# Weight-block sums of the seven-product chunks made by accumulating transfers instead of VectorE; parameter rows on GpSimd's queue; chunk 6 transposed two products later

## The reference, cut to what matters

```
def swiglu(h, w_gate, w_up, w_down):
    return (jax.nn.silu(h @ w_gate) * (h @ w_up)) @ w_down
for layer in range(DEPTH):
    x = x + 0.5 * swiglu(rmsnorm(x, norm_g[layer, 0]), ffn_w_gate[layer, 0], ffn_w_up[layer, 0], ffn_w_down[layer, 0])
    x = x + hybrid_mixer(rmsnorm(x, norm_g[layer, 1]), ...)
    x = x + 0.5 * swiglu(rmsnorm(x, norm_g[layer, 2]), ffn_w_gate[layer, 1], ffn_w_up[layer, 1], ffn_w_down[layer, 1])
```

## Time and profile before

| | |
|---|---|
| median of three runs | 2633.23 us |
| profiled execution, its own time | 2632.9 us |
| its span in the trace | 2631.2 us |
| TensorE busy | 2583.8 us, 98% |
| VectorE busy | 1801.3 us, 68% |
| ScalarE busy | 1555.4 us, 59% |
| GpSimd busy | 833.4 us, 32% |
| SyncE's DMA queue | 443.25 MB, 56.2% of 16 engines' span |
| mean granted TensorE clock | 0.997 |

### The profile page before, as it was taken

The page is one execution under the profiler, slowest core; times in us unless marked ns, Lnnn a source line. Parts: engine busy times, 40 slices in busy tenths (PEclk is TensorE's granted clock), DMA queues, the critical chain, the costliest instruction groups (busy, mean ns, idle before and its releaser), DMA issues.

```text
span 2631.2 us, 42862 instructions
## 1 busy us (share of the span) xinstructions
PE 2583.8 (98%) x16554; PEld 2242.2 (85%) x16554; DVE 1801.3 (68%) x2641; ACT 1555.4 (59%) x2202; POOL 833.4 (32%) x415
## 2 busy tenths in 40 slices
PE   9999999999999998999999999999999999999999
PEld 8888998888888996888789999978878899999787
DVE  6873745877863735876876787458768767873686
ACT  5665655656565654655565645656565657456655
POOL 0007671000018671000007754720000087548100
PEclk9999999999999999999999999999999999999999
DMA  9545547547535446548547742585475487325752
GB/s 290 176 129 181 146 156 252 177 143 247 179 124 182 147 161 215 168 151 250 178 126 174 172 91 80 167 255 179 137 249 179 109 191 171 82 82 179 246 184 97
DMA packets 349166, 447.19 MB, mean 170 GB/s; under 512 B 29612, under 2 KB 238512, under 8 KB 348964
## 3 DMA queue, kind: packets, MB, share of 16 engines
q1 hardware_dynamic: 348148, 443.25, 56.2%
q10 hardware_dynamic: 816, 1.21, 0.2%
HBM read 443.31 MB, written 1.05 MB: 169 GB/s over the span
## 4 chain that ended last, share of the span: by engine, by line
PE 84%; ACT 5%; DVE 4%; SPq 2%; issue 2%; DMA 2%; POOL 0%; DVEq 0%; ACTq 0%; POOLq 0%
PE PS L614 25%; PE PS L616 25%; PE PS L615 25%; PE PS L867 1%; SPq L403 1%; ACT wp L638 1%; DMA ring<-in_ffn_w_in_dram 1%; ACT xh L1498 1%; PE PS L1288 1%; DMA ring<-in_ffn_w_up_dram 1%; PE PS L1361 1%; DVE sq L2313 1%; PE PS L1351 1%; ACT wp L674 1%; PE PS L819 1%
## 5 line engine op out<-in xcount | busy, mean ns | idle before, releaser
L646 POOL TENSOR_TENSOR wp<-ring,wp 128x1024 fp32r<-128x1024 f32 (+2 forms) x332 | 786.1, 2384 | 1482.1 <-ACT wp L638 1481.6
L638 ACT ACTIVATE wp<-ring 128x1024 fp32r<-128x1024 f32 x712 | 746.6, 1054 | 570.7 <-PE PS L614 363.5
L646 DVE TENSOR_TENSOR wp<-ring,wp 128x1024 fp32r<-128x1024 f32 x380 | 459.1, 1220 | 209.4 <-ACT wp L638 208.8
L614 PE MATMUL PS<-wp,xh 128*128 128x512 f32 (+2 forms) x1440 | 568.2, 395 | 14.5 <-DVE wp L646 13.3
L616 PE MATMUL PS<-wp,xl 128*128 128x512 f32 (+2 forms) x1440 | 558.3, 388 | 0.0
L615 PE MATMUL PS<-wp,xh 128*128 128x512 f32 (+2 forms) x1312 | 507.6, 387 | 0.0
L614 PE MATMUL PS<-xh,wp 128*128 128x256 f32 x1536 | 445.0, 290 | 0.8 <-POOL wp L646 0.7
L616 PE MATMUL PS<-xh,wp 128*128 128x256 f32 x1536 | 434.4, 283 | 0.0
L615 PE MATMUL PS<-xl,wp 128*128 128x256 f32 x1536 | 434.3, 283 | 0.0
L614 PEld LDWEIGHTS PS<-wp,xh 128*128 128x128 f32 x1440 | 270.9, 188 | 78.4 <-DVE wp L646 17.9
L614 PE MATMUL PS<-wp,hh 128*128 128x512 f32 x832 | 328.4, 395 | 0.0
(11 more groups left out here) (342 smaller groups left out, 3508.0 us busy)
## 6 DMA issues: line engine op xcount, KB each, us to landing
ring<-in_mix_w_in_dram SPq DMA_DIRECT2D x256, 256.0 KB, 3.8
ring<-in_ffn_w_in_dram SPq DMA_DIRECT2D x224, 256.0 KB, 3.5
ring<-in_ffn_w_down_dram SPq DMA_DIRECT2D x176, 256.0 KB, 3.6
ring<-in_w_in_dram SPq DMA_DIRECT2D x176, 256.0 KB, 3.0
ring<-in_ffn_w_out_dram SPq DMA_DIRECT2D x176, 256.0 KB, 3.8
W<-in_ffn_w_in_dram SPq DMA_DIRECT2D x64, 512.0 KB, 6.9
ring<-in_ffn_w_gate_dram SPq DMA_DIRECT2D x112, 256.0 KB, 3.2
ring<-in_ffn_w_up_dram SPq DMA_DIRECT2D x112, 256.0 KB, 3.8
```

The costliest lines, as they stand in the source:

```text
L614: first_ = mm(o, w[0], x[0], start=start, stop=False, skip_group_check=True)
L638: act_(dst, src, ACT.Copy).then_inc(hi_ready, 1)
L646: (engine or v_).tensor_tensor(dst, src, part_views(t, wh)[0], ALU.subtract).then_inc(lo[t.slot()], 1)
```

## The change

The four subtractions L2313 go from VectorE. In their place ScalarE makes a negated copy of b11 in t1's buffer and of b22 in t2's (`negated`, two operations of 128x2048 in each pair), and GpSimd's queue issues four accumulating transfers of 1 MB within on-chip memory in each pair (`pool_sums`), each of which waits for the one before: t1 = -b11 + b12; then b12's buffer becomes t3 = b12 - b22; then t2 = -b22 + t1; then, once both halves of the low part of M6 are made, the same buffer becomes t4 = t2 + b21. The signs of t2 and t3 are turned, and those of the activations' sums with them. t4's own buffer goes. The four sums now have semaphores of their own, on which the high parts wait.

The negated copies of the first pair stand on ScalarE in the rounds of chunks 3 and 4, those of the second pair after down tiles 6 and 8. SyncE's wait before block b21 is now for M4. `load_params2` goes to GpSimd's queue, after the low parts of the last mixer of the first block and before the sums of that feed-forward's first pair; the sums of its second pair stand behind GpSimd's constants, so behind the wait for L1442's transposes. `turn(PLAIN - 1)` stands between M3 and M7 and ScalarE's and VectorE's `turned(c - 1)` behind the high and low parts of M2.

```
 def two_chunks(p):                                   # TensorE
                 product("M5", sum_part(1, 1), True)
-                if p == 0:
-                    turn(PLAIN - 1)
...
                 product("M3", sum_part(1, 0))
+                if p == 0:
+                    turn(PLAIN - 1)
...
+            def negated(p, dst, src):                 # ScalarE
+                e.wait_ge(blocks_in[src], blocks_landed(s, p))
+                act_(raw[dst], raw[src], ACT.Copy, scale=-1.0).then_inc(ff[1].sem, ff[1].did(f"{tag}.{dst}n.{p}"))
...
                 chunk(c)
+                if c == 3:
+                    negated(0, "t1", "b11")
                 if c == 4:
                     sums_high()
                 high(e, t, 2)
+                if c == 4:
+                    negated(0, "t2", "b22")
...
-            high(e, t, 4)
+            high(e, t, 2)
+            negated(1, "t1", "b11")
+            high(e, t, 2)
+            negated(1, "t2", "b22")
...
             low_whole(0, "M1")                        # VectorE
             turned(PLAIN - 2)
-            low_whole(0, "M5", "T2")
-            block3(0)
-            block4(0)
+            low_whole(0, "M5")
             two_chunks(0, *PAIRS[0])
...
+        def pool_sums(e, t, ff, s, tag, p):           # GpSimd
+            at = blocks_landed(s, p)
+            add = lambda n, dst, src: e.dma_start(raw[dst], raw[src], accum_op=ALU.add).then_inc(summed_in[n], 16)
+            t.k = PAIR_AT[p]
+            e.wait_ge(ff[1].sem, ff[1].at(f"{tag}.t1n.{p}"))
+            e.wait_ge(blocks_in["b12"], at)
+            add("t1", "t1", "b12")
+            e.wait_ge(ff[1].sem, ff[1].at(f"{tag}.t2n.{p}"))
+            e.wait_ge(summed_in["t1"], at // 2)
+            add("t3", "b12", "t2")
+            e.wait_ge(summed_in["t3"], at // 2)
+            add("t2", "t2", "t1")
+            e.wait_ge(summed_in["t2"], at // 2)
+            e.wait_ge(blocks_in["b21"], at)
+            for i in range(2):
+                low_ready(e, t, SUM_OF["M6"] + i)
+            add("t4", "t2", "b21")
...
             e.wait_ge(first["mix"][2].sem, first["mix"][2].at("mc3"))
+            load_params2(e)
+            pool_sums(e, f1, ff, stage1(lay, 2), "f1", 0)
             ok(p_.memset(tmask[:], 0.0))
...
                 ok(p_.memset(DU["U", c][half[1], :, half[0]], 0.0), "masks" if c == 1 else None)
+            pool_sums(e, f1, ff, stage1(lay, 2), "f1", 1)
```

More of the change, by code:

```diff
@@ L445, in pair_block @@
                     sp.wait_ge(track_[0].sem, track_[0].at(f"{tag_}.{product}.{p_}", lay_))
-                    if name == "b21":
-                        sp.wait_ge(track_[2].sem, track_[2].at(f"{tag_}.T4.{p_}", lay_))
                 load_block(sp, p, name, gate, up)
-            blocks = (("b11", "M1"), ("b12", "M7"), ("b22", "M3"), ("b21", "M2"))
+            blocks = (("b11", "M1"), ("b12", "M7"), ("b22", "M3"), ("b21", "M4"))
             for c in range(PLAIN):
@@ L506, in _ @@
                                 load_tile(sp, t, a[key][lay][c * P:(c + 1) * P, :])
-                    def between(last=lay == LAYERS - 1 and half == 1):
-                        if last:
-                            load_params2(sp)
                     load_ffn(sp, t, first["ffn"], f"f{half}", lay, kmajor(a["ffn_w_gate"][lay, half]),
                              kmajor(a["ffn_w_up"][lay, half]), a["ffn_w_down"][lay, half],
-                             (first["mix"], lay) if half == 1 else None, before, between)
+                             (first["mix"], lay) if half == 1 else None, before, lambda: None)
                     before = (first["ffn"], f"f{half}", lay, 1)
@@ L657, in sum_ready @@
             else:
-                e.wait_ge(ff[2].sem, ff[2].at(f"{tag}.{RAW_OF[n].upper()}.{p}"))
+                e.wait_ge(summed_in[RAW_OF[n]], blocks_landed(s, p) // 2)
         def by_planes(ap):
@@ L2293, in sums3 @@
                 own("S1")
-                v_.tensor_tensor(sq[:, front, q1], sq[:, front, q0], sq[:, front, q1], ALU.subtract).then_inc(
+                v_.tensor_tensor(sq[:, front, q1], sq[:, front, q1], sq[:, front, q0], ALU.subtract).then_inc(
                     ff[2].sem, ff[2].did(f"{tag}.S3"))
@@ L2298, in sums2 @@
                 own("S3")
-                v_.tensor_tensor(sq[:, front, q0], sq[:, back, q1], sq[:, front, q0], ALU.subtract).then_inc(
+                v_.tensor_tensor(sq[:, front, q0], sq[:, front, q0], sq[:, back, q1], ALU.subtract).then_inc(
                     ff[2].sem, ff[2].did(f"{tag}.S2"))
@@ L2303, in sums4 @@
                 own("S2")
-                v_.tensor_tensor(sq[:, back, q0], sq[:, back, q0], sq[:, front, q0], ALU.subtract).then_inc(
+                v_.tensor_tensor(sq[:, back, q0], sq[:, back, q0], sq[:, front, q0], ALU.add).then_inc(
                     ff[2].sem, ff[2].did(f"{tag}.S4"))
@@ L2310, in sums_low, with low_whole @@
                     ff[2].sem, ff[2].did(f"{tag}.sl{i}"))
[L2312 to L2339, removed]
+            def low_whole(p, n):
+                if n == "M5":
+                    e.wait_ge(summed_in["t2"], blocks_landed(s, p) // 2)
                 low_sum(e, t, n).then_inc(lo[t.slot(SUM_OF[n])], 1)
@@ L2401, in dve_ffn @@
                 chunk(c)
[L2402 to L2412, removed]
+            low(e, t, FRONT - 5)
+            low_whole(1, "M1")
+            low_whole(1, "M5")
             two_chunks(1, *PAIRS[1])
@@ L2960, in _ @@
             env.lay = 0
+        def pool_sums(e, t, ff, s, tag, p):
[15 more added lines that the diff above has]
+            add("t4", "t2", "b21")
         def pool_mix2(e, t):
+            ff = second["ffn"]
             low(e, t, 4 if env.lay else 2, nc.gpsimd)
+            for p in range(len(PAIRS)):
+                pool_sums(e, t, ff, stage2(env.lay, 0), "f0", p)
             t.k = FFN_TILES
@@ L2990, in pool_mix2 @@
             low(e, t, 3 * KB - AHEAD + 4, nc.gpsimd)
+            t.k = T2 - FFN_TILES
+            f1 = Tiles(t.number())
+            for p in range(len(PAIRS)):
+                pool_sums(e, f1, ff, stage2(env.lay, 2), "f1", p)
         @block.gpsimd
@@ L3016, in _ @@
                     low(e, t, 2, nc.gpsimd)
+                ff, f1 = first["ffn"], Tiles((lay + 1) * T1 - FFN_TILES)
+                for p in range(len(PAIRS)):
+                    pool_sums(e, t, ff, stage1(lay, 0), "f0", p)
                 t.k = FFN_TILES
                 low(e, t, T1 - 2 * FFN_TILES + 2, nc.gpsimd)
+                if lay < LAYERS - 1:
+                    for p in range(len(PAIRS)):
+                        pool_sums(e, f1, ff, stage1(lay, 2), "f1", p)
             e.wait_ge(first["mix"][2].sem, first["mix"][2].at("mc3"))
+            load_params2(e)
+            pool_sums(e, f1, ff, stage1(lay, 2), "f1", 0)
             ok(p_.memset(tmask[:], 0.0))
```

29 lines of the change are left out of this document (15 added, 14 removed).

## The result

The changed kernel takes 2677.4 us (median of 4 runs, 2675.9 to 2690.7) against 2633.4; the ratio is 1.0171 with a 95% interval of 1.0139 to 1.0203. It is slower by 44 us where I forecast 15 us faster.

The account below looks back on a forecast made before the run. The prediction took TensorE to bound the kernel, busy 2583.8 of 2631.2 us. Its sum was 2632.9 - 11.8 - 14.3 + 5 + 4 + 2 = 2617.8, said as 2618 us, range 2606 to 2665, likeliest case 2613 to 2628.

Parts of the forecast that it names:

- What can be won: TensorE's waits at chunk 6's transposes (11.8 us) and the gap from SyncE's parameter rows (14.3 us): 26.1 us together.
- The 1.48 us go even if the transposes stayed: Chunk 6, eight feed-forwards: without two VectorE subtractions, `gated` ends early enough to end each wait, 11.8 us in all.
- 5 + 4: Second pairs: 5 us lost over eight feed-forwards to slow transfers, 4 us more in the first block's last one.
- First pair ... Loss 0: First pairs, before M4: t4 has 10.3 us, from 93.7 to 104.0, and may take 10, so nothing is lost.
- The clock: TensorE's granted clock falls behind long gaps; expected with transfers at 11 us, no term in the sum.
- rival A: Accumulating transfers too slow, TensorE waits before M6 and M4 of the second pairs: slower, 2655 at 9.6 us each; chance 0.28.
- The price L of a transfer: Time of one 1 MB accumulating transfer: 7.9 us alone, 8.6 beside the weights, with 5 and 11 kept as bounds.
- 4L - 33.1: Loss in each second pair: four transfers against 33.1 us of room before M4; forecast 0.6 us each, 5 in all.
- The late chain behind GpSimd's constants: First block's last feed-forward: the second pair's sums start behind GpSimd's two constants, costing 4 us more.
- break-even of 8.3: Mean transfer time in us over a second pair's four, from which rival A decides.
- C: Parameter rows do as much harm from GpSimd's queue, so only 11.8 us are gained: 2630, no change; chance 0.09.
- D: VectorE keeps GpSimd from preparing transfers, starts up to 2.3 us late, 10.2 us each at worst: 2675; chance 0.04.

Follow-up runs that it names:

- params_only: The kernel before with one edit, the 28 parameter rows moved from SyncE's queue to GpSimd's: 2620.8 us, 0.9952.
- plain_copies: The changed kernel with its 64 accumulating transfers made plain copies, additions left out, so a price and no result: 2606.4 us, 0.9894.
- sums_earlier_turn_first: As sums_earlier, but chunk 6's transposes stay between M5 and M6 as in the kernel before: 2608.4 us, 0.9903.
- params_turn: The kernel before with parameter rows on GpSimd's queue and chunk 6's transposes between M3 and M7, all sums still on VectorE: 2618.0 us, 0.9938.
- sums_earlier: params_turn with the first pair's four sums made earlier on VectorE, in the rounds of chunks 3 to 5, no transfers: 2609.2 us, 0.9905.
- b11_late: The changed kernel, but SyncE asks for the second pair's b11 only when the first pair's t4 has landed: 2677.3 us, 1.0161.
- gpsimd_sums: The kernel before with both small edits (params_turn), the first pair's t3 and t4 made by GpSimd subtraction instructions, no transfers: 2651.9 us, 1.0068.
- t4_on_vector: The changed kernel with t4 made by VectorE in both pairs; t1, t3 and t2 stay transfers: 2671.5 us, 1.0145.
- chain_earlier: t4_on_vector with the second pair's negated copies one step earlier on ScalarE: 2643.7 us, 1.0035.
- first_pair_only: The changed kernel with only the first pair's t1, t3 and t2 as transfers; its t4 and the second pair's sums on VectorE: 2611.7 us, 0.9913.

## Why the prediction was wrong, by its steps

**What can be won: right.** 26.1 us were read from the waits, 14.3 and 11.8. params_only has 12.9 of the first with 2 of cost foreseen, plain_copies is within 1 us of 2606.8 (28.7 us under the kernel before that ran beside it), and sums_earlier_turn_first reaches 25 without any transfer. "The 1.48 us go even if the transposes stayed" holds too. That they come from VectorE being full between M5 and M6 is shown by params_turn and sums_earlier: moving the transposes gave 2 to 3 us, emptying the stretch 9 more.

**Where the loss lies.** The profiled executions of the change and of plain_copies are 84 us apart. TensorE's waits make 53.8 of them (69.3 against 15.5): in the change 28.9 us in front of M4 in the first pairs, and 21.1 in front of M5 and 1.6 in front of M4 in the second. Its busy time makes the other 30.6 (2610.7 against 2580.1). For these three my sum had 0, 5 + 4, and nothing.

**"First pair ... Loss 0": the step that failed most.** I gave t4 there up to 10 us of 10.3. It was issued at 95.28, not 93.7, because t3 and t2 before it took 10.0 and 9.5 us, not 8.6 each, and t2 landed 1.2 us late; t4 itself took 11.1, and up to 12.4 in the others. The gap before M4 is 2.6 to 4.5 us in each feed-forward. b11_late shows that the loads beside t4 are the cause of its own length.

**The clock: named in rival A, charged nowhere in the forecast; this term at nothing failed too.** I had the 0.60 of the earlier trace rows behind 11.34 us and 1.00 behind 1.48 and put no price on what lies between. In the change the 1.2 GHz level came behind 14 of the 16 gaps, for 3 to 6 us each; it did not behind the two of 1.47 and 2.00 us, nor behind one of 3.41 in gpsimd_sums. Each us of the added waits came with 0.6 us of added busy time (30.6 to 53.8), so losses of this size should have been multiplied by about 1.6.

**The price L of a transfer: too low by 0.3 us, and not the main miss.** I took 7.9 us alone and 8.6 beside the weights, 8.4 in the mean of a second pair's four. Alone it is better, 7.0; beside weights it is 9.3, and the mean of the four is 8.7. I had let the weights "give way" and added 0.7, with the engines at 0.59 to 0.66 for weights; a transfer's own engine time, now measured, is 5.4 us (0.129 x 2689 / 64) and has to find its place beside that. By my own rule L = 8.7 costs 4L - 33.1, 1.8 us in each second pair, 14 in place of 5: about 2627, inside my range. The rule is roughly right: in the first feed-forward four transfers are 35.0 us, about 1.6 more lie between landing and next issue, against 33.1, so 3.5 us; measured 2.0 before M5 and 0.8 before M4. I had not seen that VectorE's wait for t2 stands in front of M5's low part, so the loss shows at M5 and not at M6, and M6's low part comes 2.2 us later. The wait is needed: M5's low part is written over t1, which the transfer that makes t2 reads (`sum_lows` and `W` are one memory). m5_unbound, which has no such wait, gave no time, so what it costs by itself is open.

**The late chain behind GpSimd's constants: right.** 4 us were foreseen; that feed-forward's gap before M5 is 5.33 us, against 1.5 to 3.3 in the others.

**The rivals.** A has the right place and sign, but not by its own sum: with the L that was measured it gives 2627, and the 2677 lie above even its edge of 2665, since first pairs and clock are missing there as well. Its 0.28 was too low, for the forecast's own mean L of 8.4 was already past the break-even of 8.3. C did not come: params_only is at 0.9952. Nothing speaks for D: the second pairs' plain copies of t4 land in 4.5 to 4.7 us with VectorE at work beside them.

**What was not foreseen at all** is that the two losses are one. When the chain starts hangs on ScalarE and, ahead of it, on the down tiles' DMA; what it costs hangs on when TensorE arrives. t4_on_vector and b11_late each took a loss of 2.6 to 4.5 us away in the first pair and found most of it again in the second; only chain_earlier, which moves the start, and first_pair_only, which takes the transfers out of the second pairs, bring it back.

## What to carry to other kernels

When an engine is off the path by its average, look for the stretch in which it is full, and first try to move its work to where the same engine is free: one edit of the order did here what 64 transfers should have. An addition in a transfer cost twice a copy in engine time here, so compare a chain of them with its window at the load of that window, and leave it a margin. And charge a wait of TensorE with what the clock adds behind it.

## What the runs showed of the hardware

- An accumulating transfer of 1 MB within on-chip memory takes 1.93 times the DMA engine time of a copy (12.9% of 2688.9 us against 6.9% of 2604.9 for 64). It lands in 6.9 to 7.1 us alone, in 9.3 in the median, and in 11.1 to 12.4 beside a block and down tiles; copies in 4.5 to 4.7 alone and 6.5 in the median. Its issue holds GpSimd for 0.86 us, a copy's for 0.53.
- TensorE's granted clock stayed at 1.00 behind gaps of 1.48 and 2.00 us, was 0.50 for about 3 us behind one of 2.59 and one of 2.04, and for up to 6 us behind one of 4.54; behind one of 3.41 in gpsimd_sums it stayed at 1.00.
- GpSimd and VectorE subtracting in the same memory: 4.87 us for a subtraction of 1.22 us on VectorE, 6.66 for one of 2.29, and 5.5 for GpSimd's own.
